# Stick-breaking heads in a fused encoder layer: the mask of later keys moves from TensorE products to GpSimd fills and a 0/1 factor in the scan

## The reference

```python
causal = key_pos[None, :] < t[:, None]
z = jnp.einsum('bqhd,bshd->bhqs', qb, k).astype(jnp.float32) * dh ** -0.5
log_keep = jnp.where(causal, jax.nn.log_sigmoid(-z), 0.0)
log_w = jax.nn.log_sigmoid(z) + lax.cumsum(log_keep, axis=3, reverse=True) - log_keep
a = jnp.where(causal, jnp.exp(log_w), 0.0)
return jnp.einsum('bhqs,bshd->bqhd', a.astype(v.dtype), v)
```

## Time and profile before

| | |
|---|---|
| median of 3 runs | 843.1 us (842.61 to 844.68) |
| the profiled execution, its own time | 842.65 us |
| its span, first to last instruction | 840.8 us |
| TensorE busy | 831.5 us, 99% |
| VectorE busy | 509.4 us, 61% |
| ScalarE busy | 353.8 us, 42% |
| GpSimd busy | 30.8 us, 4% |
| mean granted TensorE clock | 0.997 of full |

### The profile page before, as it was taken

How to read it: one execution, slowest core, us unless ns; L and a number is a source line. 1 busy time by engine, 2 the same in 40 slices (tenths; PEclk the granted TensorE clock), 3 DMA queues, 4 the chain that set the end, 5 groups by cost and what they waited for, 6 DMA issues and landing times.

```text
span 840.8 us, 10539 instructions
## 1 busy us (share of the span) xinstructions
PE 831.5 (99%) x4067; PEld 699.7 (83%) x4067; DVE 509.4 (61%) x861; ACT 353.8 (42%) x557; POOL 30.8 (4%) x75
## 2 busy tenths in 40 slices
PE   9999999999999999999999999999999999999996
PEld 6888889888888888888888998888888888888885
DVE  5549889898789888685653877433333433222237
ACT  6545656775555536525423632222222222211122
POOL 1710000000000000000000001000000000000000
PEclk9999999999999999999999999999999999999998
DMA  8352122112222221222262224222222222222202
GB/s 271 126 207 101 54 97 101 51 51 101 68 84 71 80 101 55 97 101 83 72 251 97 64 88 157 94 101 100 100 100 100 100 100 100 101 101 101 100 1 100
DMA packets 15816, 84.51 MB, mean 101 GB/s; under 512 B 1808, under 2 KB 3860, under 8 KB 7072
## 3 DMA queue, kind: packets, MB, share of 16 engines
q1 hardware_dynamic: 13472, 76.89, 25.8%
q0 software_dynamic: 2016, 6.86, 2.4%
q10 hardware_dynamic: 288, 0.20, 0.1%
HBM read 81.82 MB, written 2.13 MB: 100 GB/s over the span
## 4 chain that ended last, share of the span: by engine, by line
PE 96%; DVE 2%; ACT 1%; issue 0%; DVEq 0%; ACTq 0%
PE bank L1334 65%; PE bank L1551 19%; PE bank L1614 3%; PE bank L1381 2%; PE bank L1475 2%; PE bank L1462 2%; PE bank L1439 1%; PE bank L1441 1%; PE bank L1520 0%; PE bank L1482 0%; DVE probsT L1044 0%; DVE sel L942 0%; DVE probs L1047 0%; ACT w_hi L532 0%; DVE result L1281 0%
## 5 line engine op out<-in xcount | busy, mean ns | idle before, releaser
L865 DVE TENSOR_TENSOR w_lo<-raw,w_hi 128x2048 fp32r<-128x2048 f32 x65 | 149.0, 2292 | 131.1 <-ACT w_hi L532 108.5
L1334 PE MATMUL bank<-x_lo,w_hi 128*128 128x512 f32 x688 | 174.6, 391 | 0.0
L1334 PE MATMUL bank<-x_hi,w_hi 128*128 128x512 f32 x688 | 171.4, 391 | 0.0
L1334 PE MATMUL bank<-x_hi,w_lo 128*128 128x512 f32 x688 | 170.5, 389 | 0.0
L1334 PEld LDWEIGHTS bank<-x_hi,w_lo 128*128 128x128 f32 x688 | 129.0, 188 | 26.9
L1334 PEld LDWEIGHTS bank<-x_hi,w_hi 128*128 128x128 f32 x688 | 128.0, 188 | 26.0
L1334 PEld LDWEIGHTS bank<-x_lo,w_hi 128*128 128x128 f32 x688 | 127.8, 188 | 25.8
L532 ACT ACTIVATE w_hi<-raw 128x2048 fp32r<-128x2048 f32 x45 | 86.4, 1919 | 94.9 <-PE bank L1551 85.5
L1551 PE MATMUL bank<-w_lo,h_hi 128*128 128x512 f32 x176 | 56.8, 389 | 0.0
L1551 PE MATMUL bank<-w_hi,h_lo 128*128 128x512 f32 x176 | 56.8, 389 | 0.0
L1551 PE MATMUL bank<-w_hi,h_hi 128*128 128x512 f32 x176 | 56.8, 389 | 0.0
(11 more groups left out here) (306 smaller groups left out, 1107.5 us busy)
## 6 DMA issues: line engine op xcount, KB each, us to landing
raw<-in_stream SPq DMA_DIRECT2D x67, 1024.0 KB, 4.8
resid<-in_x POOLq DMA_DIRECT2D x1, 2048.0 KB, 8.2
xraw<-in_xT SPq DMA_DIRECT2D x6, 256.0 KB, 5.3
out<-result SPq DMA_DIRECT2D x3, 512.0 KB, 2.6
early_raw<-in_stream SPq DMA_DIRECT2D x1, 1024.0 KB, 9.5
bias_b<-bias_vectors POOLq DMA_DIRECT2D x1, 1024.0 KB, 6.5
bias_a<-bias_vectors POOLq DMA_DIRECT2D x1, 1024.0 KB, 9.8
ln_g<-in_g POOLq DMA_DIRECT2D x2, 512.0 KB, 7.5
```

The lines of the kernel that those rows point to most:

```text
L865: dve.tensor_tensor(w_lo[:, s, :], raw[:, s, :], w_hi[:, s, :].bitcast(f32), ALU.subtract).then_inc(lo_ready, 1)
L1334: ins = pe.matmul(dst, lhs[a](k), rhs[b](k), start=n == 0, stop=n == n_all - 1)
```

## The change

1. The queries of the D heads are multiplied by the scale 1/8 when they are split into their two parts (ScalarE's copy gets a scale, VectorE's subtraction becomes one instruction that scales and subtracts), so the scores in PSUM are already scaled and later instructions drop the factor.
2. The products that added -1e30 (line 1444: four per head, sixteen in all) are gone, and with them the two constants.
3. VectorE no longer writes max(z, 0) while ScalarE is at the logarithm. It waits for the logarithm of a bank and then writes max(z, 0) + log(...) in one instruction (`stick_sums`); there are three per head.
4. GpSimd, which waits for each of these (`soft_sum_ready`), overwrites the later keys of the diagonal blocks in `probs` by 1e30 (`affine_select`: 128, 256 and 128 columns for the three banks). VectorE's scans wait for it (`hidden_keys`).
5. The scan was state = (probs + state) + probsT. It is now state = earlier * state + probs, where `earlier` is a constant tile of ones with zeros at later keys, built by GpSimd at the start; the zeros keep the 1e30 of later keys out of the sum over the others. The subtraction after it is a plain one.

```diff
@@ gpsimd @@
-            pool.memset(ident_bf[:], 0.0)
-            pool.memset(not_causal[:], 0.0)
+            pool.memset(earlier[:], 1.0)
...
+            pool.wait_ge(bias_ready, 1)
+            for d in range(HEADS):
+                for b, tiles in enumerate(((3,), (2, 0), (1,))):
+                    first = min(score_place("D", r)[1] + P * r for r in tiles)
+                    blocks = probs[:, 512 * b + first:512 * b + first + P * len(tiles)]
+                    if len(tiles) > 1:
+                        blocks = blocks.rearrange("p (r k) -> p r k", k=P)
+                    pool.wait_ge(soft_sum_ready, 3 * d + b + 1)
+                    pool.affine_select(out=blocks, in_=blocks, compare_op=ALU.is_gt, fill=-NEG, base=0,
+                                       pattern=[[0, len(tiles)], [-1, P]] if len(tiles) > 1 else [[-1, P]],
+                                       channel_multiplier=1).then_inc(hidden_keys, 1)
@@ scalar: stick_log, stack_high @@
-                    act.activation(probsT[:, b * 512:b * 512 + w], score[b][:, 0:w], ACT.Abs, scale=SCALE).then_inc(abs_ready, 1)
+                    act.activation(probsT[:, b * 512:b * 512 + w], score[b][:, 0:w], ACT.Abs).then_inc(abs_ready, 1)
...
-                last = act.activation(q_stack[rows, :], q[rows, :], ACT.Copy)
+                last = act.activation(q_stack[rows, :], q[rows, :], ACT.Copy, scale=SCALE if kind == "D" else 1.0)
@@ vector: stick_relu becomes stick_sums @@
-                    dve.wait_ge(abs_ready, 3 * d_before(n) + b + 1)
-                    step(dve.tensor_scalar(probs[:, b * 512:b * 512 + w], score[b][:, 0:w], SCALE, 0.0, ALU.mult, ALU.max))
-                step_wait()
+                    whole = slice(b * 512, b * 512 + w)
+                    dve.wait_ge(soft_ready, 3 * d + b + 1)
+                    dve.scalar_tensor_tensor(probs[:, whole], score[b][:, 0:w], 0.0, probsT[:, whole], ALU.max,
+                                             ALU.add).then_inc(soft_sum_ready, 1)
@@ vector: stick_scan @@
-                    dve.wait_ge(soft_ready, 3 * d + b + 1)
+                    dve.wait_ge(hidden_keys, 3 * d + b + 1)
...
-                        step(dve.tensor_tensor_scan(probsT[:, s][:, ::-1], probs[:, s][:, ::-1], probsT[:, s][:, ::-1], 0.0,
-                                                    ALU.add, ALU.add))
+                        step(dve.tensor_tensor_scan(probsT[:, s][:, ::-1], earlier[:, SEQ - width:][:, ::-1],
+                                                    probs[:, s][:, ::-1], 0.0, ALU.mult, ALU.add))
                     step_wait()
-                    dve.scalar_tensor_tensor(probs[:, whole], score[b][:, 0:w], SCALE, probsT[:, whole], ALU.mult,
-                                             ALU.subtract).then_inc(log_ready, 1)
+                    dve.tensor_tensor(probs[:, whole], score[b][:, 0:w], probsT[:, whole], ALU.subtract).then_inc(log_ready, 1)
@@ vector: the slot of a D head @@
-                    stick_relu(now)
                     value_low(now)
+                    stick_sums(now)
                     stick_scan(now)
@@ tensor: unit_scores @@
-                        if kind == "D":
-                            ins = pe.matmul(score[b][:, col + P * r:col + P * (r + 1)], not_causal[:], ident_bf[:], start=False,
-                                            stop=True, skip_group_check=True)
```

More of the change, by code:

```diff
@@ L229, in layer_program @@
     ident = at("ident", M, [P, P], f32)
-    ident_bf = at("ident_bf", M + 512, [P, P], bf16)
-    not_causal = at("not_causal", M + 768, [P, P], bf16)
+    earlier = at("earlier", R + 116 * K, [P, SEQ], f32)
     small = M + 1024
@@ L330, in layer_program @@
         part_mean_ready, end_sum_ready = sem("part_mean_ready"), sem("end_sum_ready")
+        soft_sum_ready, hidden_keys = sem("soft_sum_ready"), sem("hidden_keys")
         part_squares_ready, rest_var_ready = sem("part_squares_ready"), sem("rest_var_ready")
@@ L447, in _ @@
             step_wait()
[L448 to L452, removed]
+            pool.affine_select(out=ident[:], in_=ident[:], compare_op=ALU.not_equal, fill=1.0, base=0,
+                               pattern=[[-1, P]], channel_multiplier=1)
+            pool.affine_select(out=earlier[:, SEQ - P - 1:], in_=earlier[:, SEQ - P - 1:], compare_op=ALU.is_gt, fill=0.0, base=0,
+                               pattern=[[-1, P + 1]], channel_multiplier=1).then_inc(consts_ready, 1)
             pool.wait_ge(x_loaded[-1], 16)
@@ L903, in stack_low @@
                 dve.wait_ge(stack_hi_ready, n + 1)
-                last = dve.tensor_tensor(q_stack[others, :], q[rows, :], q_stack[rows, :].bitcast(f32), ALU.subtract)
+                if kind == "D":
+                    last = dve.scalar_tensor_tensor(q_stack[others, :], q[rows, :], SCALE, q_stack[rows, :].bitcast(f32),
+                                                    ALU.mult, ALU.subtract)
+                else:
+                    last = dve.tensor_tensor(q_stack[others, :], q[rows, :], q_stack[rows, :].bitcast(f32), ALU.subtract)
                 if new_keys(kind, h):
@@ L1022, in softmax_unit, with stick_sums @@
                 last.then_inc(probs_ready, 1)
-            def stick_relu(n):
-                if d_before(n) == 0:
+            def stick_sums(n):
+                d = d_before(n)
+                if d == 0:
                     dve.wait_ge(index_used, 3 * HEADS)
+                    dve.wait_ge(consts_ready, 1)
                 for b in range(3):
                     w = bank_width("D", b)
-                    dve.wait_ge(abs_ready, 3 * d_before(n) + b + 1)
-                    step(dve.tensor_scalar(probs[:, b * 512:b * 512 + w], score[b][:, 0:w], SCALE, 0.0, ALU.mult, ALU.max))
-                step_wait()
+                    whole = slice(b * 512, b * 512 + w)
+                    dve.wait_ge(soft_ready, 3 * d + b + 1)
+                    dve.scalar_tensor_tensor(probs[:, whole], score[b][:, 0:w], 0.0, probsT[:, whole], ALU.max,
+                                             ALU.add).then_inc(soft_sum_ready, 1)
             def stick_scan(n):
@@ L1438, in unit_scores @@
                         queries, dst = slice(P * r, P * (r + 1)), score[b][:, col:col + width]
-                        pe.matmul(dst, q_stack[:, queries], k_stack[:, k0:k0 + width], start=True, stop=False,
-                                  skip_group_check=kind == "D")
-                        ins = pe.matmul(dst, q_stack[:, queries], k_low[:, k0:k0 + width], start=False, stop=kind != "D",
-                                        skip_group_check=kind == "D")
-                        if kind == "D":
-                            ins = pe.matmul(score[b][:, col + P * r:col + P * (r + 1)], not_causal[:], ident_bf[:], start=False,
-                                            stop=True, skip_group_check=True)
+                        pe.matmul(dst, q_stack[:, queries], k_stack[:, k0:k0 + width], start=True, stop=False)
+                        ins = pe.matmul(dst, q_stack[:, queries], k_low[:, k0:k0 + width], start=False, stop=True)
                     ins.then_inc(scores_done, 1)
```

1 line of the change is left out of this document (removed).

## The result

The changed kernel takes 846.6 us (median of 9 executions, 845.11 to 847.11) against 843.09 (842.61 to 844.68, 9 executions): a ratio of 1.0036 [1.0028, 1.0045], so 3.5 us slower by the medians.

A forecast was written before the change was run, and what follows sets the result against it. TensorE bounds the kernel, but the VectorE-ScalarE D chain sets slot 13's start. Four heads at 0.9 us longer, less 0.52 and 0.10 taken up, give +2.98 us: 843.1 + 3.0 = 846.1 us, range 844.0 to 848.6.

The forecast's parts named there:

- TensorE's saving, 0.36 us a head: D heads' scores on TensorE: removing sixteen mask products saves 0.09 us each, 1.44 us over four heads, spent in waits.
- Sums without cover, 0.71 us a head: VectorE in each D head: sums of 1.61 us now follow bank 0's logarithm, so the first scan starts 0.71 us later.
- Multiply and add cost a scan nothing: VectorE's scans: multiply and add take as long as add and add, 1.21 us for 512 columns; extra cost 0.
- Fills, 0.2 us a head: GpSimd's fills beside VectorE's scans: shared SBUF access lengthens each head by 0.2 us, between 0 and 0.6.
- nothing: Rival on the fills: they cost nothing, a head is 0.71 us longer, 2.22 us in all, 845.3 us; chance 0.2.
- dear: Rival on the fills: scans wait on each, a head is 1.3 to 1.8 us longer, 847.7 to 849.7 us; chance 0.17.
- Taken up on the way, 0.62 us: ScalarE's waits for TensorE absorb lateness of the chain: 0.52 us after slot 6 and 0.10 us after slot 8.
- TensorE's waits 0.7, 1.4 and 2.5 us: TensorE waits for low weights in slot 9 (0.7 us) and slot 11 (1.4), and for the exp at slot 13 (2.5).
- The chain's end, +2.98 us: The exp of slot 12's head, awaited by slot 13's transposes, ends 2.98 us later than before.
- Slot 13's wait leaves the clock alone: TensorE behind slot 13's wait: the granted clock was assumed not to fall; named only as a failure condition, without size.
- The chain has slack: Rival: links after slots 8 and 10 give back 0.7 us or more a head; 841.7 to 843.1 us; chance 0.13.

The follow-up runs named there:

- experiment 2: The changed kernel without GpSimd's fills and without the waits for them, later keys not masked: 845.78 us, ratio 1.0031.
- experiment 3: The changed kernel with each GpSimd fill replaced by a memset of the whole diagonal blocks, which reads nothing: 846.19 us, ratio 1.0036.
- experiment 4: The kernel before, mask products kept and no fills, but with sums behind the logarithm, the scan over a tile of ones and scaled queries: 845.34 us against 842.89.
- experiment 8: The changed kernel with ScalarE doing the logarithms of banks 0 and 1 before bank 2, whose sum follows the first scan and subtraction: 842.4 us, ratio 0.9995.

## Why the prediction was right, and where it was not

The forecast was 846.1 us, slower, and 846.6 was measured. Step by step:

- **TensorE's saving, 0.36 us a head.** The score distance came out as the predicted 1.26 us, and what was saved was swallowed by waits, as stated. But 0.36 was too small: it is 0.46, or 1.86 for 1.44 in all. The distance was cut at the start of the first product behind the last mask product. TensorE starts that one 0.03 us behind the mask product and then needs longer for it: the group of seven at 75.25 took 1.86 us before, the same seven at 154.80 take 1.78 now, which is 0.08 of the missing 0.10. A distance between two instructions of one kind, past the place, would have had it. Since the chain set the end, the error cost the forecast nothing.
- **Sums without cover, 0.71 us a head.** 0.69 measured, by experiments 2, 3 and 4 alike.
- **Multiply and add cost a scan nothing.** Right: 1.21 to 1.22 us for 512 columns in experiments 2 to 4. The prediction named the half-throughput rule of the Trainium skill (DVE: opcode table, instruction layouts, handler registers and perf-mode slots, section 6) beside this term; the rows agree with it as far as they go, with 1.21 us for either pair of operations.
- **Fills, 0.2 us a head.** 0.16 measured, and by the named mechanism: the scan is held behind a fill that reads SBUF, and the last fill ends just behind the scan. The 0.3 that the prediction got for a scan that waits out the whole fill was too much. The two rivals on their price fall: nothing (experiment 2 differs) and dear (head 0.85 longer, not 1.3).
- **Taken up on the way, 0.62 us.** 0.82: 4 x 0.85 = 3.4 us of length came out as 2.58 at the end. This term was mis-sized. The prediction counted only ScalarE's idle time ahead of emptying the tile, 0.52 and 0.10. But those starts can also move forward into the end of the exp ahead. In the kernel after, slot 6:

```profile
84.38 0.42 ACT L613 ACTIVATE probs<-probs 128x256 f32<-128x256 f32 x1 [0.42 <-DVE probs L1064]
84.70 0.58 ACT L573 ACTIVATE qk_a<-bank 128x512 f32<-128x512 f32 x1
```

  From start to start it is 0.32 us, where it was 83.48 to 84.42 = 0.94: 0.62 taken up. After slot 8 it is 111.55 to 111.88 = 0.33 where it was 0.52: 0.2. Together 0.8.
- **TensorE's waits 0.7, 1.4 and 2.5 us.** 0.6, 1.19 and 2.34.
- **The chain's end, +2.98 us.** +2.58. Of the 0.40 too much, 0.2 are the take-up above and 0.2 the heads, four times 0.85 where 0.9 was taken.
- **Slot 13's wait leaves the clock alone.** This is the step that failed. It stood in the text only as what would make the forecast wrong, without a term or a chance. Behind 2.3 us of standing the granted clock fell in the profiled executions of the kernel after to 0.66 and 0.71 over 5 us, at a cost of 1.5 to 1.6 us, and by their times some 9 of 16 executions had it.

So 846.1 came close partly by luck, because two errors cancel: the chain alone gives, on the profiled execution's own time, 842.65 + 2.6 = 845.25, and there the lower group lies (845.1 to 845.4); the clock adds 1.5 us in the other executions, and the median is one of them. "The chain has slack" is refuted: lateness grew from head to head up to 2.42. Slack exists only if the order is changed, as experiment 8 did.

What stays open is what decides whether the clock falls in a given execution, and whether the ten transposes behind the stand have a part in it: they follow the stand in every run that has one.

## What to carry to other kernels

Before taking work from the busiest engine, find its next wait and ask when that data will be there: here TensorE arrived 0.18 us ahead of the chain, so of 1.86 us removed 0.6 to 0.8 were won, and the way to gain was to shorten the chain as well (840.45 us). When an operation is merged with a later one, ask under what it lay before: the three sums cost VectorE as much as the old max(z, 0), yet moving them behind the logarithm cost 0.69 us in each head, four times in a row. And a new wait in front of TensorE, 2.2 to 2.3 us long here, is to be priced with the clock behind it, in part of the executions.

## What was not expected of the hardware

- Nine products that nobody needs made the kernel faster, 0.7 us by the medians on one chip (845.46 against 846.19): the granted clock stayed at 1.00 where it had been 0.71. Four did the same, with 1.44 us of standing left.
- The clock didn't fall while TensorE stood. It stood from 163.8 to 166.16 at the full clock and fell as the transposes began, in the other trace of the same kernel 1 us after they had begun, and then stayed at 1.2 GHz under work without a gap for over 3 us.
- The fall doesn't come each time. The same program with 2.2 us of standing had 1.00 in one profiled execution (experiment 2), while 2.2 to 2.3 us gave 0.66 or 0.71 in three others.
- A bf16 product of 128 columns between fp32 ones cost TensorE 0.116 us (1.86 / 16), of which the start of the next instruction shows 0.09.
- A wait shown as 0.18 us of idle time cost 0.34 us from start to start: a product's row of 0.39 us reaches over the start of the next, 0.22 us after its own in the scores of slot 6, so the idle time behind the last of them comes out too small.
- Setting 256 and then 128 columns by memset took 0.53 us on GpSimd beside a running scan; reading and filling them took 1.57, and held the scan 0.17.
